# A depthwise convolution of 31 taps on TensorE: column-tiled diagonals, or full matmuls over 16 channels by 8 token phases

## The reference

```python
def trunk_layer(x, ...):
    x = layer_norm(ALPHA * x + 0.5 * swiglu(x, f1_wg, f1_wu, f1_wd), ln_f1_g, ln_f1_b)
    m, new_a, new_b = token_mixers(x, ctx_a, ctx_b, w_in, b_in, ...)
    x = layer_norm(ALPHA * x + m, ln_mix_g, ln_mix_b)
    x = layer_norm(ALPHA * x + 0.5 * swiglu(x, f2_wg, f2_wu, f2_wd), ln_f2_g, ln_f2_b)

def token_mixers(h, ...):
    a_val, a_gate, g_b, g_c, b_val = split(h @ w_in + b_in)   # 5 x 512 columns
    u = a_val * sigmoid(a_gate)
    ua = causal depthwise conv of u, 31 taps, per channel (512 channels)
    ua = silu(layer_norm(ua + b_dw_a, ln_conv_g, ln_conv_b))  # norm over the 512 channels
    v = g_c * b_val;  ub = g_b * (causal depthwise conv of v, 3 taps)
    return concat(ua, ub) @ w_o + b_o, ...
```

## Time and profile before

| | |
|---|---|
| time, median of 3 runs (lowest, highest) | 1201.17 us (1199.64, 1202.07) |
| the profiled execution: time, span of the slowest core | 1196.67 us, 1194.5 us |
| spans of the eight cores | 1191.3 to 1194.5 us |
| granted TensorE clock, mean of each core | 0.997 to 0.999 |
| TensorE busy | 1174.6 us of the span |
| stages (us from the span's start) | mixing of block 0 from 481, of block 1 from 565.7, FFN2 from about 689 |

### The profile page before, as it was taken

How to read it: one execution, slowest core, us unless ns; L and a number is a source line. 1 busy time by engine, 2 the same in 40 slices (tenths; PEclk the granted TensorE clock), 3 DMA queues, 4 the chain that set the end, 5 groups by cost and what they waited for, 6 DMA issues and landing times.

```text
span 1194.5 us, 18723 instructions; the slowest of 8 cores (1191.3 to 1194.5 us)
## 1 busy us (share of the span) xinstructions
PE 1174.6 (98%) x6844; PEld 620.1 (52%) x6844; DVE 552.2 (46%) x863; ACT 199.6 (17%) x360; POOL 145.6 (12%) x211
## 2 busy tenths in 40 slices
PE   7999999999999999999999999999999999999997
PEld 4444444466666544444655555444444466666443
DVE  1122217743222388445877845577225432222485
ACT  1111110012122000221532223122100012122000
POOL 1111111110000012000211012111101100000010
PEclk9999999999999999999999999999999999999999
DMA  9888976459444245796598779578953374442132
GB/s 158 134 139 172 182 106 141 125 125 167 82 72 71 36 116 153 110 239 150 116 210 210 163 144 159 114 195 150 199 116 113 89 144 86 72 71 36 36 126 89
DMA packets 83289, 152.82 MB, mean 128 GB/s; under 512 B 40032, under 2 KB 42720, under 8 KB 83184
## 3 DMA queue, kind: packets, MB, share of 16 engines
q0 software_dynamic: 26736, 73.97, 39.0%
q1 hardware_dynamic: 56464, 77.66, 23.9%
HBM read 189.45 MB, written 28.64 MB: 183 GB/s over the span
## 4 chain that ended last, share of the span: by engine, by line
PE 84%; DVE 7%; DMA 4%; issue 3%; ACT 1%; SPq 1%; POOL 0%; DVEq 0%; ACTq 0%; POOLq 0%
PE ps L582 55%; PE ps L566 26%; DMA sb_xq<-xk 2%; PE ps L835 2%; DMA sb_xT<-xpq 1%; DVE sb_stt L488 1%; DVE sb_xq L478 1%; DVE sb_xq L512 1%; PE ps L675 1%; DVE sb_xq L482 1%; DVE sb_RH L603 0%; DVE sb_sttc L962 0%; DVE sb_RH L978 0%; PE ps L954 0%; DVE sb_RW L891 0%
## 5 line engine op out<-in xcount | busy, mean ns | idle before, releaser
L582 PE MATMUL ps<-sb_xT,sb_ring 128*128 128x347 bf16 (+3 forms) x4384 | 767.2, 336 | 8.7 <-DMA sb_xT<-xpq 6.1
L582 PEld LDWEIGHTS ps<-sb_xT,sb_ring 128*128 128x128 bf16 x4384 | 426.9, 98 | 339.0 <-issue 18.7
L603 DVE TENSOR_TENSOR sb_RH<-sb_sg,ps 128x347 bf16<-128x347 f32 (+3 forms) x224 | 129.3, 577 | 444.7 <-ACT sb_sg L601 439.6
L566 PE MATMUL ps<-sb_RW,sb_RH 128*128 128x512 bf16 x1364 | 295.6, 379 | 0.6 <-DVE sb_xq L482 0.6
L601 ACT ACTIVATE sb_sg<-ps 128x347 f32<-128x347 f32 (+3 forms) x224 | 114.1, 509 | 657.8 <-PE ps L582 645.8
L566 PEld LDWEIGHTS ps<-sb_RW,sb_RH 128*128 128x128 bf16 x1364 | 133.2, 98 | 161.9 <-issue 1.9
L461 POOL TENSOR_TENSOR sb_mv<-sb_mv,sb_neghalf 128x1 f32<-128x1 f32 (+1 forms) x47 | 52.5, 1117 | 449.0 <-DVE sb_mv L459 449.0
L478 DVE SCALAR_TENSOR_TENSOR sb_xq<-sb_xq,ps 128x1024 f32<-128x1024 f32 (+1 forms) x50 | 60.9, 1218 | 91.9 <-PE ps L566 82.6
L401 POOL DMA_DIRECT2D sb_ring<-wgu x87 | 47.4, 545 | 412.0 <-PE ps L582 411.5
L519 DVE SCALAR_TENSOR_TENSOR sb_xq<-sb_xq,sb_mv,sb_lnb 128x1024 f32<-128x1024 f32 (+1 forms) x50 | 64.2, 1283 | 11.4 <-POOL sb_mv L461 6.2
L488 DVE BATCH_NORM_STATS2 sb_stt<-sb_xq 128x6 f32<-128x512 f32 (+1 forms) x100 | 64.2, 683 | 3.5
(11 more groups left out here) (75 smaller groups left out, 288.7 us busy)
## 6 DMA issues: line engine op xcount, KB each, us to landing
sb_ring<-wgu POOLq DMA_DIRECT2D x87, 512.0 KB, 7.2
xk<-sb_xq SPq DMA_DIRECT2D x32, 512.0 KB, 4.4
sb_xq<-xk SPq DMA_DIRECT2D x32, 512.0 KB, 6.4
sb_RW<-wd POOLq DMA_DIRECT2D x22, 512.0 KB, 10.7
sb_RH<-uscr SPq DMA_DIRECT2D x32, 263.0 KB, 8.9
sb_xq<-xp SPq DMA_DIRECT2D x16, 512.0 KB, 4.5
sb_ring<-win POOLq DMA_DIRECT2D x16, 512.0 KB, 5.7
yp<-sb_xq SPq DMA_DIRECT2D x15, 512.0 KB, 2.9
```

The lines of the kernel that those rows point to most:

```text
L566: ins = e.matmul(ps[:n, bank(yb + h)], lhsT=lhs(f), rhs=rhs(f, h), start=(f == 0), stop=(f == nk - 1))
L582: ins = e.matmul(out, lhsT=ring[:, slot, cw:cw + 128], rhs=xT_rhs(b, k, tok0, n), start=(k == 0), stop=(k == KC - 1))
L603: P.op("dve", lambda e: e.tensor_tensor(out=hT[:, f, tok0:tok0 + n], in0=sg[:, p_ % 2, :n], in1=ps[:, bu * 512: bu * 512 + n], op=ALU.mult ...
```

## The change

The 31-tap conv is made with full 128 x 128 matmuls. A partition of the moving operand is one of 16 channels at one of 8 shifts, an output partition one of the same 16 channels at one of 8 token phases (token modulo 8); columns are 128 groups of 8 tokens. `U_bf` is stored by phase: the product of an `a_item` is written with elements of one phase together, neighbours in time 264 bytes apart. `rep_out` writes it as it lies, `rep_in` is one DMA per chunk, with rows of 264 bytes and no overlap.

`conv(i)` (i = 0 to 7 in each block) is 4 groups x 5 column offsets of 128 x 128 matmuls with 128 columns. Its weights, 20 x 128 columns, are built per i in one of three buffers: from compact taps `wv` times a mask of channels, either by VectorE in two `piece`s of 1280 elements, or by ScalarE in four `part`s of four ACTIVATEs of 160 elements. In block 0, i = 0 to 5 are VectorE's (items 4 to 14), 6 and 7 ScalarE's (items 14 to 17); ScalarE also builds i = 2, 0, 1 of block 1 at items 18 to 23, and i = 3 to 7 in block 1's items 13 to 29. `out` takes four ACTIVATEs of 128 columns (the bias differs by group), `flip` transposes the result (four fp32 transposes) two items after the conv, and `put` copies it on ScalarE from PSUM to `Z`, so that `Z[:, q, :]` holds the 128 tokens of phase q with all 512 channels.

The norm runs on these rows of one phase: statistics, gain and shift read `Z` in SBUF, without the fp32 transposes (except for the sample tile); the copy to `cat` writes every eighth token. So `s3` of any tile waits for all eight copies. Block 0's steps move to items 22, 23 and 0 to 9, `wo` matmuls of block 0 to items 10, 12, 14, 16, 19, 22, 24, 27 (from 8, 10, 12, 15, 18, 21, 24, 27), and convs in block 1 to 12, 14, 16, 18, 21, 24, 27, 30 (from 14, 15, 20, 21, 26, 27, 34, 35). Steps of block 1 start at FFN2's item 0 instead of 2. Block 1's token groups are 352, 344 and 344 columns. The pool queue loads `wv` (128 x 1280) in FFN1 where SP loaded the identity stack `E4`.

```diff
@@ -272,25 +272,29 @@
-        U_bf = RH[:, 0:4 * UW].rearrange("p (c t) -> p c t", c=4)
-        R2 = RH[:, 4 * UW:4 * UW + 8 * R2W].rearrange("p (s g t) -> p s g t", s=2, g=4)
...
+        U_bf = RH[:, 0:4 * UW].rearrange("p (c s m) -> p c s m", c=4, s=8)
+        R2 = RH[:, 4 * UW:6 * UW].rearrange("p (l g m) -> p l g m", l=2, g=8)
...
+        accP = RHF[:, o:o + 1536].rearrange("p (l t) -> p l t", l=3)
...
+        Z = RHF[:, o:o + 4096].rearrange("p (q c) -> p q c", q=8)
@@ -355,7 +359,7 @@
-            return [(0, 512), (512, 512)] if b == 0 else [(0, 347), (347, 347), (694, NTB[1] - 694)]
+            return [(0, 512), (512, 512)] if b == 0 else [(0, 352), (352, 344), (696, NTB[1] - 696)]
@@ -445,7 +449,7 @@
-            P.op("sp", lambda e: e.dma_start(out=E4[:], in_=estkd), writes=["E4"], dma="c_e4")
+            P.op("pool", lambda e: e.dma_start(out=wv[:], in_=wvd), writes=["wv"], dma="c_wv")
@@ -771,19 +775,20 @@
-                                dst = U_bf[:, ch, 30 + t_:30 + t_ + m]
+                                dst = U_bf[:, ch, :, 4 + t_ // 8:4 + (t_ + m) // 8].rearrange("p s m -> p m s")
...
+                                ab = [v.rearrange("p (m s) -> p m s", s=8) for v in (sg[:, p_ % 2, o_:o_ + m], vb[:, p_, o_:o_ + m])]
...
-                            P.op("dve", lambda e, m=m, o_=o_, dst=dst: e.scalar_tensor_tensor(
-                                out=dst, in0=sg[:, p_ % 2, o_:o_ + m], scalar=1.0, in1=vb[:, p_, o_:o_ + m],
-                                op0=ALU.add, op1=ALU.mult),
+                                ab = [sg[:, p_ % 2, o_:o_ + m], vb[:, p_, o_:o_ + m]]
+                            P.op("dve", lambda e, dst=dst, ab=ab: e.scalar_tensor_tensor(
+                                out=dst, in0=ab[0], scalar=1.0, in1=ab[1], op0=ALU.add, op1=ALU.mult),
@@ -800,50 +805,82 @@
         def a_begin(b):
...
-            P.op("dve", lambda e: e.tensor_copy(out=U_bf[:, :, 0:30], in_=halo[:, :, 0:30]),
+            P.op("dve", lambda e: e.tensor_copy(out=U_bf[:, :, :, 0:4].rearrange("p c s m -> p c m s"),
+                                                in_=halo[:, :, 0:32].rearrange("p c (m s) -> p c m s", s=8)),
...
         def rep_out(b, ch):
-            P.op("sp", lambda e: e.dma_start(out=uscr[ch], in_=U_bf[:, ch, :]),
...
+            P.op("sp", lambda e: e.dma_start(out=uscr[ch].rearrange("(p x) -> p x", p=128),
+                                             in_=U_bf[:, ch, :, :].rearrange("p s m -> p (s m)")),
...
         def rep_in(ch):
...
-            src = uscr[ch].rearrange("(g c) t -> c g t", g=4)
-            for q in range(4):
-                P.op("sp", lambda e, q=q: e.dma_start(out=R2[32 * q:32 * q + 32, sl, :, :], in_=src[:, :, q:q + R2W]),
-                     reads=[("uscr", ch)], writes=[("R2", sl, q)], dma="r2_%d_%d" % (sl, q))
-
-        def conv_w(ch):
...
-            P.op("dve", lambda e: e.tensor_tensor(
-                out=dgb[:, ch, :].rearrange("p (q g c) -> p q g c", q=8, g=4),
-                in0=E4[:, :, :].unsqueeze(1).to_broadcast([128, 8, 4, 32]),
...
-                op=ALU.mult), reads=["E4", "cst", "warm"], writes=[("dgb", ch)])
-
-        def conv(ch, h, bk):
-            sl = ch % 2
+            src = uscr[ch].rearrange("(g q m) -> q g m", g=8, q=128)
+            P.op("sp", lambda e: e.dma_start(out=R2[:, sl, :, :], in_=src), reads=[("uscr", ch)], writes=[("R2", sl)],
+                 dma="r2_%d" % sl)
+
+
+        def conv_w(i):
+            sl = i % 3
+            out = wcs[sl].rearrange("p (a c q) -> p a c q", a=20, c=16)
+            src = wv[:, i, :].rearrange("p (a q) -> p a q", q=8)
+
+            def part(h):
+                def f(e):
+                    ins = None
+                    for c in range(4 * h, 4 * h + 4):
+                        ins = e.activation(out=out[:, :, c, :], in_=src, func=AF.Identity, scale=cc(C_MK + c))
+                    return ins
+                P.op("act", f, reads=["wv", "cst", "warm"], writes=[("wc", sl, h)])
+
+            def piece(h):
+                P.op("dve", lambda e: e.tensor_tensor(
+                    out=out[:, 10 * h:10 * h + 10], in0=src[:, 10 * h:10 * h + 10].unsqueeze(2).to_broadcast([128, 10, 16, 8]),
+                    in1=cst[:, C_MK:C_MK + 16].unsqueeze(1).unsqueeze(3).to_broadcast([128, 10, 16, 8]), op=ALU.mult),
+                    reads=["wv", "cst", "warm"], writes=[("wc", sl, 2 * h), ("wc", sl, 2 * h + 1)])
+            return [lambda h=h: part(h) for h in range(4)], [lambda h=h: piece(h) for h in range(2)]
+
+        def conv(i, bk, tbk):
+            (ch, h) = divmod(i, 2)
+            sl, ws, al = ch % 2, i % 3, i % 3
...
-                    for q in range(8):
-                        for g_ in range(4):
-                            ins = e.matmul(ps[32 * g_:32 * g_ + 32, bank(bk)],
-                                           lhsT=dgb[:, ch, q * 128 + 32 * g_: q * 128 + 32 * g_ + 32],
-                                           rhs=R2[:, sl, g_, h * 512 + 4 * q: h * 512 + 4 * q + 512],
-                                           start=(q == 0), stop=(q == 7), tile_position=(0, 32 * g_))
+                    for g in range(4):
+                        for j in range(5):
+                            a = (g * 5 + j) * 128
+                            ins = e.matmul(ps[:, bk * 512 + g * 128: bk * 512 + (g + 1) * 128], lhsT=wcs[ws][:, a:a + 128],
+                                           rhs=R2[:, sl, 4 * h + g, j:j + 128], start=(j == 0), stop=(j == 4))
...
-                P.op("pe", pe, reads=[("dgb", ch)] + [("R2", sl, q) for q in range(4)], writes=[("ps", bk)])
+                P.op("pe", pe, reads=[("wc", ws, q) for q in range(4)] + [("R2", sl)], writes=pst(bk))
...
-                     reads=[("ps", bk), "cst"], writes=[("acc", ch, h)])
-            return go, out
+                def f(e):
+                    ins = None
+                    for g in range(4):
+                        ins = e.activation(out=accP[:, al, g * 128:(g + 1) * 128], in_=ps[:, bk * 512 + g * 128: bk * 512 + (g + 1) * 128],
+                                           func=AF.Identity, bias=cc(C_BP + 4 * i + g))
+                    return ins
+                P.op("act", f, reads=list(pst(bk)) + ["cst"], writes=[("accP", al)])
+
+            def flip():
+                def pe(e):
+                    ins = None
+                    for g in range(4):
+                        ins = e.transpose(out=ps[:, tbk * 512 + g * 128: tbk * 512 + (g + 1) * 128],
+                                          in_=accP[:, al, g * 128:(g + 1) * 128], identity=ident[:, :])
+                    return ins
+                P.op("pe", pe, reads=[("accP", al), "ident"], writes=pst(tbk))
+
+            def put():
+                P.op("act", lambda e: e.activation(
+                    out=Z[:, :, i * 64:(i + 1) * 64],
+                    in_=ps[:, bank(tbk)].rearrange("p (k q) -> p q k", q=8), func=AF.Identity),
+                    reads=pst(tbk), writes=[("Zc", i)])
+            return go, out, flip, put
@@ -937,53 +974,51 @@
+            allz = [("Zc", i) for i in range(8)]
...
+                if i < 8:
+                    return
...
+                P.op("pe", pe, reads=[("aS", ch) for ch in range(4)] + ["ident"], writes=pst(4))
+
+            def at(i):
+                if i < 8:
+                    return Z[:, i, :], allz, Z[:, i, :], ("Zp", i), 128
+                return ps[:NS, bank(4)], list(pst(4)), Z[:NS, 0, :], ("Zp", 0), NS
...
             def stats(i):
...
-                P.op("dve", lambda e: e.bn_stats(out=sttc[:n, sl, :], in_=ps[:n, bank(pb)]), reads=pst(pb),
...
+                P.op("dve", lambda e: e.bn_stats(out=sttc[:n, sl, :], in_=src), reads=rt, writes=[("sttc", sl)])
...
+                P.op("act", lambda e: e.activation(out=cs[:n, q, :], in_=dst, func=AF.Silu), reads=[wt], writes=[("cs", q)])
@@ -1000,8 +1035,9 @@
+                dst = cat[b][:, 0:4, t:BLK:8] if t < 8 else cat[b][:, 0:4, tok0:tok0 + n]
...
-                    out=cat[b][:, 0:4, tok0:tok0 + n],
+                    out=dst,
@@ -1033,7 +1069,7 @@
-                P.op("pe", pe, reads=[("cat%d" % b, k, tok0) for k in range(4)]
+                P.op("pe", pe, reads=[("cat%d" % b, k, t0) for k in range(4) for t0 in ([BLK] if t == 8 else range(0, BLK, 128))]
@@ -1153,22 +1189,20 @@
-        spread(sides, [16, 18, 20, 22], [(lambda ch=ch: conv_w(ch)) for ch in range(4)])
...
-        def spread_conv(sides, at, banks, end=99):
-
-            j = 0
-            for ch in range(4):
-                for h in range(2):
-                    go, out = conv(ch, h, banks[j % len(banks)])
-                    spread(sides, [at[j]], [go])
-                    spread(sides, [(at[j] + 1, 0) if at[j] < end else end], [out])
-                    j += 1
-                if ch < 2:
-                    spread(sides, [at[j - 1]], [lambda ch=ch: rep_in(ch + 2)])
+        def spread_conv(sides, at, gens, banks, tbanks):
+
```

(46 more changed lines are left out.)

104 lines of the change are left out of this document (43 added, 61 removed).

## The result

The changed kernel takes 1214.34 us (median of 5 runs, 1209.39 to 1214.99) against 1199.64 (5 runs): ratio 1.0113, 95% interval 1.0092 to 1.0133. Slower by 1.1%, where I had forecast 1194.9 and put 0.17 on slower.

What follows compares the result with a forecast made beforehand. TensorE was taken as the bound, VectorE close behind in block 1. Terms -13.6 + 3.7 + 0 + 2.6 + 1.0 = -6.3 us gave span 1188.2, carried over to 1194.9 us; range 1186.5 to 1203.0.

Steps and rivals of the forecast that it cites:

- The convolution: TensorE, both mixing blocks: a conv takes 1.10 us instead of 1.95, so 16 convs save 13.6 us.
- Rival 4: TensorE's convs: weight loads aren't hidden, 98 ns a matmul, +0.2 instead of -13.6 us, total 1205.7; chance 0.05.
- The product in the head: Head of block 1: VectorE's strided product takes 0.7 us, rounds 3.1 against TensorE's 2.58, costing 2.6 us (bounds 1.6, 4.4).
- Rival 3: Element-wise strides cost double everywhere: product 1.04 us, five puts 1.2 instead of 0.6; 1201.0, no change; chance 0.15.
- The border stall: End of block 0: ScalarE's backlog of weight parts (1.16 us each) stalls TensorE 3.7 us entering block 1 (bounds 1, 12).
- Rival 2: ScalarE's weight building at block 0's end: a part takes 1.8 us, 19 add 12 us, total 1207.1; chance 0.10.
- rival 1: Queues don't bind: ScalarE's passes 0.26 us, no strided-product penalty, VectorE's waits overlap; all 13.6 us arrive, 1187.6; chance 0.18.
- The head without the strided writes: Head of block 1: five rounds in which VectorE's 3.1 us exceeds TensorE's 2.58, 2.6 us in all.
- The tail: End of block 1: VectorE's 14.8 us against TensorE's 15.0, conv 7's out behind a cast; 1.0 us added (bounds -1, 3).
- a sign of being wrong: Among the named signs that the forecast would be wrong: a flip that waits for its out; no size given.
- Block 0: First mixing block: TensorE's work falls by 3.3 us, 84.7 to 81.4; VectorE's pieces cost 0 (bounds 0, 1.5).
- what costs nothing: Transfers and queues: fewer rep_in DMAs, 24 fewer SP issues, the wv load and the new token groups; no time added.

Runs made afterwards that it cites:

- e5: Kernel before with only its conv matmuls exchanged for the 20 full 128 x 128 ones per conv (output meaningless); 1191.6 us, ratio to before 0.9936.
- e3: Changed kernel with VectorE's product and ScalarE's copy to cat both written in runs (wrong token order); 1201.0 us, ratio to before 0.9995.
- e4: Changed kernel made complete without the two strided writes, strides moved to PSUM reads, weight loads and row transfers; 1197.3 us, ratio to before 1.0000.

## Why the prediction was wrong, step by step

- **The convolution**: right. 1.12 us and no extra for the item behind it, 13.1 us of TensorE's work gone (I had 13.6). Rival 4 falls. That all of it would arrive was too much: alone it brings 8 (e5).
- **The product in the head**: the failing step. I bounded it by "0.52 us as now and twice that" and took 0.7; it is 1.67 (2.42 for 512 columns). The upper bound was no row, only a factor of two; the sentence beside it, from the Trainium skill (Vector Engine (DVE) Microarchitecture Reference, Measured stream behaviour on trn2), had 0.75 to 1.0, which was nearer and still short: the trace has 4.7 ns per column (4.4 by the difference between 512 and 344 columns), not 1.71 to 2.5. The rounds became 3.9 to 4.7, not 3.1; mending it brings 7.2 us.
- **The copy into `cat`**: a term that was missing. The diff shows its new destination, I gave it no cost and no bound. It is 1.87 us more a tile on ScalarE, 3.9 us of the median core (4.5 where the product is mended already).
- **Rival 3** had the mechanism (elements apart cost more) and the product, but the wrong size, twice instead of 3.2 to 4.1 times, and the wrong second place, the `put` and not the copy: the `put`, a strided read of PSUM written in runs of 64 elements, costs 601 ns for 512 columns, as the copy in runs does (594 to 600). The cacheline note of the Trainium skill (SBUF — State Buffer, in Door 1: The DMA port swizzle) names the place, a new 16-byte line at each access, and there the trace has the full price. The Trainium skill says there that two hits on a line suffice for full bandwidth; the trace doesn't agree: at 8 bytes, two per line, ScalarE took 1.32 instead of 0.60.
- **The border stall**: the mechanism was right, the size short. A part is 1.275 us (four starts), not 1.16; 19 x 0.115 = 2.2 us. ScalarE's waits at TensorE are 2.62 + 0.50 + 0.47 = 3.6 us in e3 against 3.7, but VectorE's 1.38 for a g eviction at item 1, which I didn't have, comes ahead of them: 5.0 in all. That 3.6 meets 3.7 is in part luck: the longer parts alone add 2.2, and VectorE's wait gives ScalarE 1.4 us to catch up. Rival 2 (a part of 1.8) falls, and so does rival 1, by which ScalarE wouldn't bind.
- **The head without the strided writes**: e3 waits 3.7 us there, I had 2.6; every third round is 3.67 because the gate's halo and sample passes stand on VectorE in it, and I had priced one round and multiplied.
- **The tail**: 1.23 + 0.88 + 1.30 + 0.93 = 4.3 us of waits in e3 (core 5) against 1.3 before (on five of the eight cores), so 3.0 and not 1.0. The 0.93 is a `flip` that waits for its `out`, a sign of being wrong that I had named.
- **Block 0**: 82.0 us in e3, 3.2 less than before cut alike, where I had 3.3; the pieces cost nothing on TensorE, as forecast. The 1.5 us at item 10 came with the strided product.
- **The spread**: not in the sum. I carried over the 4.5 us between that execution and the median and nothing for the cores moving apart; the slowest core's distance from the median core grew from 4.1 to 7.0 us. With rows issued earlier it is 2.8. I had SP's queue among what costs nothing, for its 24 fewer DMAs.

Put together on the median core: -13.1 for the convs, +5.0 border, +3.7 head, +3.0 tail, less the 0.5 us that the head waited before, make -1.9; e3 measures -1.2. The two writes put 11.7 on top, which makes 10.5. On the slowest core it is 13.4, with the 2.9 us by which the cores moved apart. The 6.0 us of the late rows are a part of these 13.4 and not a further term: what the rows cost and what the writes cost overlap there (both writes in runs bring 13.2 by themselves, earlier rows 6.0).

So the step that failed is the head's term of 2.6 us for VectorE's product, with the copy beside it that had no term: together 11.7 us of the median core. The border and the tail are short by 1.3 and 2.0, the head by 1.1 even without the writes.

## What to carry to other kernels

For every instruction whose access pattern an edit changes, look at the destination first: bf16 written one element at a time took 4.1 times as long at 16 bytes on ScalarE and 3.5 times at 16 to 264 bytes on VectorE, while the same permutation taken as a strided PSUM read was free here. Where a diff moves a layout, list all its writers, and give each a bound from a measured row or call it unbounded. A gain on the busiest engine is worth at most what lies between it and the next: exchange only that one instruction group in the old kernel (8 us here, not 13) before the rest is built. And look at the slowest core by itself: a load issued one item earlier was worth 6 to 7.6 us in the changed kernel and nothing in the old one.

## What the runs showed of the hardware beyond that

- Price of 512 bf16 elements written with a step: 2 bytes 0.60 us, 4 bytes 0.75, 8 bytes 1.32, 16 bytes 2.45 (ScalarE from PSUM); 2 bytes 0.69, 4 bytes 0.74, 16 bytes 2.45, 128 bytes 2.45, 264 bytes 2.42 (VectorE).
- The clock: behind waits of 1.39 and 2.61 us the 16 matmuls of 344 columns took 4.17 us instead of 2.50 on core 0 of the changed kernel; behind 1.38 and 2.62 they took 2.49 on core 5 of e3, and behind the same two 4.17 on its core 0. Waits of this size came with a lower granted clock on some cores and not on others.
- 160 bf16 elements written in runs of 8 with a step of 256 bytes between runs cost 0.32 us start to start on ScalarE, near the 0.275 worked out from contiguous passes: runs of 16 bytes don't pay the price of single elements.
- Weight loads whose 128 columns lie 16 bytes apart take 143 ns instead of 98 (e4) and stay hidden behind matmuls of 512 columns: the spans of e4 and e3 agree within 0.3 us.
